# Six changes of order in the mixing of a two-layer trunk on one core, and the inverse blocks of the first layer shared between two engines

## The reference

```python
def step(S, inp):                      # branch B, one token, one direction, one head
    rt, wt, kt, vt, at, bt = inp
    sa = jnp.einsum('dbhvk,dbhk->dbhv', S, at)
    S = S * wt[..., None, :] + sa[..., :, None] * bt[..., None, :] + vt[..., :, None] * kt[..., None, :]
    y = jnp.einsum('dbhvk,dbhk->dbhv', S, rt) if emit else None
    return S, y

def short_conv(bg, cg, xin, conv_w):   # branch A
    return bg * dwconv3(cg * xin, conv_w)

def merge_branches(ya, yb, yc, gates, p):
    ga, gb, gc = jnp.split(jax.nn.sigmoid(gates), N_BRANCH, axis=-1)
    m = ga * (ya @ p['a_out_w']) + gb * (yb @ p['rwkv_out_w']) + gc * (yc @ p['attn_out_w'])
    return m @ p['w_o']

def trunk_layer(xc, xl, c, c_ctx, cos, sin, p, ctx_out):
    ...
    xl = xl + mod_l[2] * merge_branches(conv_l, rwkv_l, att_l, gate_l, p)
    xl = xl + mod_l[5] * conv_ffn(modulate(xl, p['norm2_g'], mod_l[3], mod_l[4]), p)
```

## Time and profile before

| | us |
|---|---|
| median of 3 runs | 2922.32 (2920.89 to 2923.82) |
| the profiled execution | 2925.36 |
| its span | 2923.6 |
| TensorE busy | 2845.0 |
| VectorE busy | 1269.2 |
| ScalarE busy | 722.8 |
| mixing passes, first layer | about 110 to 780 of the span |
| mixing passes, second layer | about 1863 to 2405 of the span |

### The profile page before, as it was taken

One profiled execution on the slowest core, in us unless ns is written; L12 is line 12 of the kernel. 1 busy time (PEld: TensorE's weight loads), 2 busy tenths in 40 slices (PEclk: granted clock), 3 DMA queues, 4 the chain that ended last, 5 costly groups with the idle time before them and its releaser, 6 DMA issues.

```text
span 2923.6 us, 56943 instructions
## 1 busy us (share of the span) xinstructions
PE 2845.0 (97%) x25077; PEld 1704.4 (58%) x25077; DVE 1269.2 (43%) x2571; ACT 722.8 (25%) x1431; POOL 52.0 (2%) x76
## 2 busy tenths in 40 slices
PE   7999999999999999999999999999999999999999
PEld 3555555555644444444444444666666677788887
DVE  2666656665322221133333211566666734323541
ACT  3333333332222221011111001344333322211110
POOL 1000000000000000010000000000000000000000
PEclk9999999999999999999999999999999999999999
DMA  7111111111243333234444324212111124344553
GB/s 249 54 48 40 41 47 41 39 40 40 80 116 101 99 110 94 77 112 116 138 136 134 91 76 125 70 55 58 52 51 55 47 71 118 108 127 133 153 153 119
DMA packets 499989, 264.26 MB, mean 90 GB/s; under 512 B 42864, under 2 KB 493888, under 8 KB 499232
## 3 DMA queue, kind: packets, MB, share of 16 engines
q1 hardware_dynamic: 498016, 251.58, 29.9%
q0 software_dynamic: 1728, 9.03, 0.9%
HBM read 255.33 MB, written 5.24 MB: 89 GB/s over the span
## 4 chain that ended last, share of the span: by engine, by line
PE 92%; ACT 4%; DVE 2%; issue 1%; DMA 0%; SPq 0%; DVEq 0%; ACTq 0%
PE psum L457 57%; PE psum L1103 8%; PE psum L478 3%; PE psum L697 2%; PE psum L817 1%; PE psum L803 1%; PE psum L518 1%; PE psum L923 1%; PE psum L786 1%; PE psum L911 1%; PE psum L901 1%; PE psum L853 1%; PE psum L647 1%; PE psum L687 1%; PE psum L842 1%
## 5 line engine op out<-in xcount | busy, mean ns | idle before, releaser
L457 PE MATMUL psum<-hT,strips 128*128 128x512 f32 (+1 forms) x3968 | 1446.3, 511 | 9.1 <-ACT arena L1539 7.2
L457 PEld LDWEIGHTS psum<-hT,strips 128*128 128x128 f32 x3968 | 724.1, 190 | 521.5 <-issue 445.9
L1103 PE MATMUL psum<-arena,strips 128*128 128x512 f32 (+1 forms) x704 | 227.6, 486 | 0.6 <-DVE arena L2377 0.6
L1103 PEld LDWEIGHTS psum<-arena,strips 128*128 128x128 f32 x704 | 133.7, 190 | 93.5 <-issue 83.5
L457 PE MATMUL psum<-arena,strips 128*128 128x512 f32 (+1 forms) x512 | 167.9, 486 | 2.0 <-DVE done L2251 2.0
L1867 DVE TENSOR_SCALAR arena<-arena 128x512 f32<-128x512 f32 (+1 forms) x88 | 37.0, 421 | 276.4 <-ACT arena L1728 276.3
L1728 ACT COPY arena<-psum 128x512 f32<-128x512 f32 (+1 forms) x88 | 42.2, 480 | 414.7 <-PE psum L457 398.5
L457 PEld LDWEIGHTS psum<-arena,strips 128*128 128x128 f32 x512 | 97.1, 190 | 69.9 <-issue 60.7
L2217 DVE SCALAR_TENSOR_TENSOR arena<-arena,psum 128x512 f32<-128x512 f32 (+1 forms) x32 | 17.8, 555 | 264.8 <-PE psum L457 264.8
L2377 DVE SCALAR_TENSOR_TENSOR arena<-psum,mod,arena 128x256 f32<-128x256 f32 x24 | 10.9, 481 | 194.3 <-PE psum L1103 194.3
L457 PE MATMUL psum<-conv_branch,strips 128*128 128x512 f32 (+1 forms) x256 | 85.8, 488 | 1.7 <-ACT arena L1602 1.5
(11 more groups left out here) (252 smaller groups left out, 3196.8 us busy)
## 6 DMA issues: line engine op xcount, KB each, us to landing
strips<-in_w_in_dram SPq DMA_DIRECT2D x158, 512.0 KB, 3.8
strips<-in_ffn_up_dram SPq DMA_DIRECT2D x88, 512.0 KB, 4.1
strips<-in_ada_w_dram SPq DMA_DIRECT2D x80, 512.0 KB, 3.9
strips<-in_ffn_down_dram SPq DMA_DIRECT2D x32, 512.0 KB, 3.8
arena<-in_ada_w_dram SPq DMA_DIRECT2D x4, 2048.0 KB, 14.0
strips<-in_w_in_dram SPq DMA_DIRECT2D x32, 256.0 KB, 3.4
strips<-in_a_out_w_dram SPq DMA_DIRECT2D x16, 512.0 KB, 4.0
strips<-in_rwkv_out_w_dram SPq DMA_DIRECT2D x16, 512.0 KB, 3.9
```

Of the source, the lines that this page charges most:

```text
L457: ins = mm(s.o[:, first:T], strip[:, b, k, :], rhs[:, k, first:T], k == 0, k == KT - 1)
L1103: ins = mm(s.o[:, lo:T], strip[:, b, j, :], hid[:, k, lo:T], k == 0, k == FT - 1)
```

## The change

Seven edits:

1. TensorE, every pass: the second pair product of direction 0 is issued ahead of the turned values.
2. TensorE, second layer, first pass: 13 instead of 8 columns of dense steps ahead of the half step, and 2, 2, 2 instead of 4, 4, 3 at three later places.
3. TensorE, first layer, passes 0 to 6: the dense steps ahead of the inverse blocks go from 4 columns to 2, and 2 columns come between `lrb1` and `lrb2`; the hop goes from 3.7 to 3.55.
4. TensorE, second layer: the hop goes from 2.15 to 2. In both layers the diagonal blocks of the next pass are issued ahead of the last dense steps.
5. ACT, second layer: C's copy ahead of the second `powers`.
6. ACT, second layer, first head of the attention: the first gate ahead of the first exponentials.
7. First layer, all passes: DVE copies `lrb0` and `lrb2`, ACT `lrb1` and `lrb3`. DVE does it behind `state_in(0)` and ahead of the hat steps.

```diff
--- before.py
+++ after.py
@@ -773,10 +773,12 @@
                     s = take(Q, "bonus", l, i)
                     one(PS[:, BANK_P[s.b], lo:T], tab["heads"], th[:, 2, lo:T]).then_inc(s.full[0], 1)
 
-                def through_inverse(i, ahead):
+                def through_inverse(i, ahead, steps):
 
                     pe.wait_ge(*slots["t10", l, i].freed)
                     for m in range(4):
+                        if m == 2 and ahead and wide:
+                            fill(steps, 2)
                         s = take(A, f"lrb{m}", l, i)
                         n, k0 = (P, 1) if 2 * m >= c0 else (CH, 2)
                         for d, h in HD2:
@@ -1029,36 +1031,36 @@
                     pair_products(0, 0, i)
                     turn_hats(0, i)
                     turn_hats(1, i)
+                    pair_products(0, 1, i)
                     turn_values(i)
-                    pair_products(0, 1, i)
                     fill(steps, 16 if wide or not ahead else 8)
                     if lo and ahead:
-                        fill(steps, 8)
+                        fill(steps, 8 if i else 13)
                     if i > 0:
                         head_var(i - 1)
                     half_step(i)
                     pair_products(1, 0, i)
                     bonus_sums(i)
-                    fill(steps, 10 if wide or not ahead else 4)
+                    fill(steps, 10 if wide or not ahead else 4 if i else 2)
                     corners(i)
                     pair_products(1, 1, i)
                     if ahead:
                         decay(0, i + 1)
-                    fill(steps, 6 if wide or not ahead else 4)
+                    fill(steps, 6 if wide or not ahead else 4 if i else 2)
                     if ahead:
                         decay(1, i + 1)
                     below_left(i)
                     corners_right(i)
                     value_products(i)
-                    fill(steps, 4 if wide or not ahead else 3)
+                    fill(steps, 4 if wide or not ahead else 3 if i else 2)
                     corner_below(i)
                     fill(steps, 4 if wide or not ahead else 5)
                     if ahead:
                         key_sums(i + 1)
                         gate_in(i + 1)
-                        fill(steps, 4 if wide else 2)
-                    through_inverse(i, ahead)
-                    hop = (3.7 if ahead else 4) if wide else 2.15 if ahead else 2.3
+                        fill(steps, 2)
+                    through_inverse(i, ahead, steps)
+                    hop = (3.55 if ahead else 4) if wide else 2 if ahead else 2.3
                     for c in range(NCH):
                         state_in(c, i)
                         if c > 0:
@@ -1066,9 +1068,9 @@
                         if c < NCH - 1:
                             state_out(c, i)
                             fill(steps, hop)
-                    fill(steps, everything)
                     if ahead:
                         diagonal_blocks(i + 1)
+                    fill(steps, everything)
                     outputs(i)
                 attend()
                 merged_out()
@@ -1521,8 +1523,8 @@
                         act.copy(MV[:, 2 * j:2 * j + 2].rearrange("p m d h t -> p (m d h t)"), PS[:, BANK_A[s.b], :])\
                            .then_inc(s.free, 1)
 
-                def through_inverse(i):
-                    for m in range(4):
+                def through_inverse(i, ms):
+                    for m in ms:
                         s = filled(f"lrb{m}", i)
                         k0 = 1 if 2 * m >= lo // CH else 2
                         n = (3 - k0) * 4 * CH
@@ -1616,8 +1618,11 @@
                             picked_rows(l, 1)
                         if t > 0:
                             weighted(t - 1, 1)
+                        if lo and t == 0:
+                            gate(0, t)
                         exps(t, 0)
-                        gate(0, t)
+                        if lo == 0 or t > 0:
+                            gate(0, t)
                         if lo == 0:
                             probs(t, 2)
                         if t == 4 and ATT_ADA[l]:
@@ -1684,12 +1689,12 @@
                         keys(1)
                     corner_below(i)
                     if ahead:
-                        powers(1, i + 1)
                         if lo:
                             conv_gate(i + 1)
+                        powers(1, i + 1)
                         key_norm(i + 1)
                         gate_in(i + 1)
-                    through_inverse(i)
+                    through_inverse(i, (1, 3) if lo == 0 else range(4))
                     if ahead:
                         if lo == 0:
                             conv_gate(i + 1)
@@ -2122,6 +2127,16 @@
                     s = filled("bonus", i)
                     tt(bon[:, lo:T], PS[:, BANK_P[s.b], lo:T], rkv[:, 2, lo:T], MUL).then_inc(s.free, 1)
 
+                def through_inverse(i, ms):
+                    for m in ms:
+                        s = filled(f"lrb{m}", i)
+                        k0 = 1 if 2 * m >= c0 else 2
+                        n = (3 - k0) * 4 * CH
+                        for p in range(2):
+                            ins = dve.tensor_copy(EE[rows(p), k0:3, m // 2, :, :, 2 * (m % 2) + p].rearrange("p k d h t -> p k (d h) t").rearrange("p k q t -> p q k t"),
+                                                  PS[rows(p), BANK_A[s.b], 0:n].rearrange("p (q k t) -> p q k t", q=4, t=CH))
+                        ins.then_inc(s.free, 1)
+
                 def state_in(c, i):
                     r = rows(c % 2)
                     add = MV[r, c // 2].rearrange("p d h t -> p h d t")
@@ -2315,6 +2330,8 @@
                         s = taps(1, "k", i + 1, 0, 1)
                         key_squares(i + 1, s)
                     state_in(0, i)
+                    if lo == 0:
+                        through_inverse(i, (0, 2))
                     steps = hats(i + 1) if ahead else iter(())
                     for _ in range(EARLY_HATS):
                         next(steps, None)
```

## The result

Before, run beside the changed kernel: 2923.82 us (median of 5, 2920.89 to 2926.15). Changed: **2936.26 us** (median of 5, 2935.68 to 2936.98). Ratio 1.0044, 95% interval 1.0031 to 1.0056: slower by more than the 0.2% that can be told from no change, 3 us above the forecast of 2933.

A forecast was written before the change was run, and what follows sets the result against it. TensorE, 97% busy, was taken as the bound, so only its waits and clock could move the time. The six edit terms summed to +3.0 us, clock falls added 8: 11 us slower, 2933 us, range 2917 to 2946.

The forecast's parts named there:

- Part 6: First layer, shared inverse copies: a new 2.4 us wait at state in, +1.6 us per pass, +10.9 in all.
- Part 7: First layer: the clock falls behind half of the seven new waits, 2.4 us each: +8 us, bounds 0 and 24.
- part 1: All 16 passes, pair product ahead of the turned values: covers a 0.28 us wait for ACT, -4.4 us.
- Part 3: Second layer, first gate ahead of the first exponentials: a 1.5 us wait on ACT goes, -1.3 us.
- Part 2: Second layer, first pass, more dense steps: 2.3 of 2.82 us wait and clock fall go, later pieces covered; -5.7 us.
- Part 4: Second layer, C's copy ahead of second powers: 0.73 us wait goes, 0.6 comes at the inverse; -2.1 us, seven passes.
- Part 5: Second layer, shorter hops, diagonal blocks earlier: 0.21 plus 0.6 us per pass, +5.6; +1.5 if DVE kept up.
- (c): First layer: DVE isn't late at state in; 2909 us, or 2917 if half so; chance 0.13, whole or half.
- (a): First layer: the waits come but the clock holds behind all seven; +3, 2925 us; chance 0.25.
- (b): First layer: the clock falls behind nearly every wait; +24, 2946 us; chance 0.17 together with (d).
- (d): New waits, for instance for ACT in the middle of the blocks: +5 on any case; chance 0.17 with (b).

The follow-up runs named there:

- e3: The changed kernel with four of the six hat steps ahead of the first state out moved further on, first layer; 2909.6 us, 0.9949 of before.
- g2: e3 with ACT copying all four inverse blocks of the first layer, as before the change; 2908.5 us, 0.9951 of before.
- f3: e3 with the second layer's hops as before (2.15, diagonal blocks behind the last dense steps); 2908.8 us, 0.9952 of before.
- g1: The changed kernel with two early hat steps instead of four ahead of the first state product, first layer; 2919.5 us, 0.9981 of before.
- g3: The kernel before with only the second pair product moved ahead of the turned values, all 16 passes; 2920.4 us, 0.9983 of before.
- f1: e3 with the second layer's first dense steps as before the change (8 columns, later 4, 4, 3); 2912.0 us, 0.9963 of before.
- f2: e3 with 10 columns of dense steps instead of 13 in the second layer's first pass, then 4, 3, 2; 2910.3 us, 0.9959 of before.
- f4: e3 with ACT's second powers ahead of C's copy again in the second layer; 2913.1 us, 0.9969 of before.

## Why the prediction was right, step by step

The forecast lay 3 us under the result, and the mechanism that decides it, a wait behind DVE's copies and clock falls behind the wait, is the one that the runs show. That the total came so near is luck in part: the first layer came out 4 us cheaper than forecast, the second 5.5 us dearer.

**Part 6 (sharing), right within 0.2 us per pass.** Predicted: a wait of 2.4 us at the state-in line in seven passes, 1.6 longer per pass, 1.3 with the pair product's 0.28 taken off. Measured: 2.59 in seven passes. A pass without a clock fall takes 84.41 us, against 83.21 before: +1.2. Without the wait (e3) it takes 82.11, 1.1 less than before, where the working's gains of 0.7 and 0.5, less 0.4 for cut pieces, with the 0.28, give 1.1. Only their cause was misread: the 0.7 belongs to the piece in the middle of the blocks, not to DVE's help (g2).

**Part 7 (the clock), right in size by two errors that nearly cancel.** I let 3.5 of seven waits bring a fall at 2.4 each, 8 us. Five did. A pass with a fall of 3.4 us took 86.0 to 86.3, some 1.7 more than one without, and the first, with 6.8 us, 87.34. Together 600.7 - 7 x 84.46 = 9.5 us. More falls, each cheaper: at half speed for 3.4 us only 1.7 are lost. The Trainium skill, page "TensorE: Matmul & The Clock Gate", section "Why this matters for your kernels", names idle gaps above about 3 us as those to avoid. These rows say that this is too high to plan by here: there were falls behind 2.59 us, and behind 1.60 (f3) and 1.74 (g1).

**What part 6 and 7 did not see, -3.3.** The kernel before has passes of 83.61, 83.97 and 85.06 us beside those of 83.21, 3.3 us in all, with "issue" stalls among their waits. In the changed kernel the first layer has no "issue" line at all. The first half step also comes 1.8 us earlier, where part 1 gives 0.3. That is mostly scatter: in the kernels built on the change, which share the code up to there, it starts at 123.9 to 129.3 us. So the first layer cost 13.1, not 17, and some 1.5 of the difference is chance.

**Part 1 (pair product), right.** L687's 4.4 us are gone, nothing took their place, and alone it gives 5 us (g3).

**Part 3 (gate), right.** From the start of attention to the next block's first products the kernel is 1.4 us shorter; predicted 1.3.

**Part 2 (first fill), the step that failed.** The 2.8 us wait went to 0.3, as said, and the clock fall behind it went. The failing step is "I take those as still covered", of the three later pieces. DVE and ACT were in time for them, but a stall of 2.7 us with no releaser came instead, with a fall of its own (from 1908.26 the changed kernel takes 3.39 us for 64 of L768). That pass is 70.25 us, 68.97 before; I had expected it shorter. f1 shows that undoing the part costs nothing from half step to half step (69.61 against 69.60), and 1.4 us by the spans. So -5.7 was about -1 at best. What f2 keeps of the part, with longer pieces behind the half step, made that pass 2.3 us shorter, without a clock fall in it, and a later pass as much longer. Why TensorE stalls stays open.

**Part 4 (C's copy), size about right in the waits.** The wait of 5.1 went, 4.8 came at the inverse blocks (predicted 0.6 a pass, measured 0.6). Undoing it (f4) costs some 0.5 to 1 us of named waits, predicted 2, and 6 in time, of which 3 are "issue" stalls.

**Part 5 (hops of layer 2), mis-sized.** The term is the 0.6 us of new waits per pass: there are 0.3 at one state product (2.2 us in seven passes). DVE did keep up in all but one place. +5.6 should have been +1.5, its lower bound, to some 3, as f3's rows say.

**The sum.** The second layer, by its rows: named waits 20.1 to 15.0 us (-5.1; this counts a wait of 0.9 us at the start of the attention, L705, which both kernels have and the stretch shown above ends short of), "issue" lines 4.3 to 8.5 (+4.2), one more piece in seven passes, 0.21 each (+1.5), the clock at half speed as long as before, 6.8 us: +0.6. From the layer's first products to L705 it takes 598.1 us before and 599.2 after, +1.1. I had expected parts 1, 2, 4 and 5 to give -4.4 there. So the first layer was 13.1 instead of 17, the second +1.1 instead of -4.4, the gate -1.4 instead of -1.3. That makes 12.8; the span grew by 11.5. The other -1.3 lies between the layers (498.2 us before, 496.9 after, from 1309.65 and 1322.65 on), where the code is the same and the clock was at half speed for 3.4 us instead of 6.8. The total is nearly the forecast's by luck.

**Rivals.** (c) is out, DVE was late in all seven; (a), no fall, and (b), a fall behind nearly every wait, lie on either side of five; (d)'s condition, new waits for ACT in the middle of the blocks, didn't appear.

## What to carry to other kernels

An engine that takes work over inherits its place in that engine's queue: count what stands between the new work and the next result that TensorE needs, not the engine's busy share (DVE is at 44%). Here 3.9 us of steps that nobody waited for stood in front of a product of 0.29 us that TensorE waited for, and moving four of the six behind it (e3) turned +0.4% into -0.5%. Where an engine that is 97% busy waits repeatedly, shorten the wait even if it can't go: half the wait took two thirds of the loss away. And before calling a shortened piece "covered", look at the same rows after the change: here the other engines were in time for it, and a stall of 2.7 us came for which the profile names no engine.

## What the runs showed of the hardware that I had not expected

- **Stalls without a releaser.** TensorE stops up to 2.7 us in the middle of small products for nothing that the profile shows, and several kernels stop at the same instruction (50 products of L733, then 9, in e3, f2 and the changed kernel; for 2.68, 0.46 and 2.68 us). In the second layer they sum to 4.3 us (before), 8.5 (after), 6.0 (e3), 4.3 (f1), 6.0 (f2), 7.3 (f3), 8.9 (f4). Most stand where hundreds of small products follow each other with little dense work between, and the changed kernel's instruction queue (q8) brings packets of 16 KB at such times, one at 1905.5, during the stall, and one at 1909.2. That TensorE outruns its supply of instructions fits this, and fits f1 and f2 at that place; no run took the fetching itself away, so the cause isn't shown. What is shown: their sum moves by up to 4 us when code moves, as much as several of the edits were worth, and by 2.5 between after and e3, whose code for TensorE is the same.
- **A clock fall behind 1.60 us** (f3) and 1.74 (g1) of idle time, and none behind 1.60 (after) and 1.77 (e3) at the same place; none behind seven waits of 1.4, eight behind fourteen waits of 2.6.
- **The copy's price on DVE**: two halves of 64 x 512 from PSUM take 1.39 us, 0.70 each; ACT takes 0.60.
